# MoE blocks of 32 slots on four column tiles instead of 64 slots on two, and adaLN products on four column tiles

## What is computed

```python
mod = jax.nn.silu(cond) @ P['ada_w'][l] + P['ada_b'][l]
...
_, eidx = lax.top_k(jnp.where(emask, sel, -jnp.inf), TOP_K)
...
hg = jnp.einsum('td,edf->tef', t, w_gate)
hu = jnp.einsum('td,edf->tef', t, w_up)
act = jax.nn.silu(hg) * hu * comb[:, :, None].astype(t.dtype)
return jnp.einsum('tef,efd->td', act, w_down).reshape(B, L, D)
```

## Time and profile before

| what | value |
|---|---|
| median of the runs | 1459.06 us |
| the profiled execution: its own time, its span | 1461.17 us, 1459.5 us |
| TensorE busy | 1210.3 us, 83% of the span |
| ScalarE, VectorE busy | 341.3 us, 362.6 us |
| MoE of layer 0, first to last matmul of the loop | 385.4 to 695.1 us |
| MoE of layer 1, first to last matmul of the loop | 1080.4 to 1418.9 us |
| DRAM traffic | 352.57 MB, mean 242 GB/s |

### The profile page before, as it was taken

How to read it: one execution, slowest core, us unless ns; L and a number is a source line. 1 busy time by engine, 2 the same in 40 slices (tenths; PEclk the granted TensorE clock), 3 DMA queues, 4 the chain that set the end, 5 groups by cost and what they waited for, 6 DMA issues and landing times.

```text
span 1459.5 us, 16823 instructions
## 1 busy us (share of the span) xinstructions
PE 1210.3 (83%) x6290; PEld 645.8 (44%) x6291; DVE 362.6 (25%) x844; ACT 341.3 (23%) x577; POOL 117.2 (8%) x183
## 2 busy tenths in 40 slices
PE   1999997896499877989799999988829999897770
PEld 0444455545255444545245553443615555453330
DVE  0310138644011000111353234444301111110006
ACT  0401013303033222333221111100303333232221
POOL 1100000002100000000120000000110000000002
PEclk9999999997699998999999997999769999999985
DMA  9984333408598999987993322223173867999963
GB/s 328 363 275 173 122 123 131 159 0 348 198 380 345 391 395 393 353 330 264 379 335 115 115 71 74 100 74 115 46 286 115 316 216 288 397 381 397 388 255 129
DMA packets 93036, 352.57 MB, mean 242 GB/s; under 512 B 7270, under 2 KB 7817, under 8 KB 84812
## 3 DMA queue, kind: packets, MB, share of 16 engines
q1 hardware_dynamic: 69396, 289.16, 52.2%
q0 software_dynamic: 14736, 48.82, 10.1%
q10 hardware_dynamic: 8872, 14.16, 2.8%
HBM read 323.24 MB, written 28.87 MB: 241 GB/s over the span
## 4 chain that ended last, share of the span: by engine, by line
PE 64%; DMA 21%; DVE 8%; issue 3%; ACT 2%; SPq 1%; POOL 1%; POOLq 0%; ACTq 0%; DVEq 0%
PE bank L728 19%; DMA ring<-in_moe_w_up_dram 14%; PE bank L560 10%; PE bank L800 9%; PE bank L742 7%; PE bank L684 6%; PE bank L514 3%; DMA ring<-in_ada_w_dram 3%; DMA slot_rows<-arena,idx 2%; PE bank L722 2%; PE bank L736 1%; DMA arena<-slot_rows 1%; PE bank L873 1%; SPq L1152 1%; PE bank L896 1%
## 5 line engine op out<-in xcount | busy, mean ns | idle before, releaser
L728 PE MATMUL bank<-ring,arena 128*64 128x256 f32 x2944 | 366.4, 405 | 66.5 <-DMA ring<-in_moe_w_up_dram 54.0
L728 PEld LDWEIGHTS bank<-ring,arena 128*64 128x64 f32 x2944 | 221.2, 146 | 213.6 <-issue 128.9
L742 PE MATMUL bank<-ring,arena 128*64 128x512 f32 x736 | 175.9, 598 | 0.0
L1125 DVE TENSOR_TENSOR arena<-arena,bank 128x128 f32<-128x128 f32 x92 | 26.5, 288 | 527.2 <-ACT arena L1044 527.2
L560 PE MATMUL bank<-ring,hT 128*128 128x512 f32 x336 | 144.9, 593 | 1.0 <-ACT hT L932 1.0
L800 PE MATMUL bank<-hT,ring 128*128 128x384 f32 x384 | 124.6, 487 | 1.0 <-ACT hT L932 1.0
L514 PE MATMUL bank<-ring,small 128*64 128x512 f32 x384 | 92.0, 634 | 32.5 <-DMA ring<-in_ada_w_dram 31.7
L560 PEld LDWEIGHTS bank<-ring,hT 128*128 128x128 f32 x336 | 63.6, 190 | 80.9 <-issue 79.7
L462 POOL DMA_DIRECT2D arena<-slot_rows x96 | 50.3, 524 | 596.2 <-PE bank L722 552.3
L800 PEld LDWEIGHTS bank<-hT,ring 128*128 128x128 f32 x384 | 72.7, 190 | 52.5 <-ACT hT L932 1.2
L1042 ACT ACTIVATE arena<-bank 128x256 f32<-128x256 f32 x92 | 35.4, 385 | 223.6 <-PE bank L728 223.3
(11 more groups left out here) (275 smaller groups left out, 964.2 us busy)
## 6 DMA issues: line engine op xcount, KB each, us to landing
ring<-in_moe_w_gate_dram SPq DMA_DIRECT2D x32, 2048.0 KB, 13.7
ring<-in_moe_w_up_dram SPq DMA_DIRECT2D x32, 2048.0 KB, 20.5
ring<-in_moe_w_down_dram SPq DMA_DIRECT2D x32, 2048.0 KB, 22.6
ring<-in_ada_w_dram SPq DMA_DIRECT2D x24, 2048.0 KB, 13.8
ring<-in_ev_w_in_dram SPq DMA_DIRECT2D x7, 2048.0 KB, 13.1
arena<-slot_rows POOLq DMA_DIRECT2D x96, 128.0 KB, 6.3
ring<-in_hy_w_in_dram SPq DMA_DIRECT2D x6, 2048.0 KB, 19.7
slot_rows<-arena ACTq DMA_DIRECT2D x92, 128.0 KB, 6.2
```

Source lines behind the costliest of these rows:

```text
L728: last = pe.matmul(bank[1 + half][side * BLK:(side + 1) * BLK, 0:HALF], slot_inT[:, k % 4, k // 4, :], w[:, k, half * HALF:(half + 1) * HA ...
L742: last = pe.matmul(bank[5][half * BLK:(half + 1) * BLK, :], act_T[:, f, :], slot4(s + 2)[:, f, half * 512:half * 512 + 512], start=f == 0, ...
```

## The change

The diff, cut to its core:

```diff
-BLK = 64
+BLK = 32
...
+    for side in range(2):
+        for s in range(BLK):
+            keep[[2 * side * BLK + s, (2 * side + 1) * BLK + s], K_SIDE + side * BLK + s] = 1
...
-            for odd in range(2):
-                pool.dma_start(gates[l, n % 2, :, odd * 512:odd * 512 + 512],
-                               mod_rows[q][odd * 64:odd * 64 + 2, :]).then_inc(gate_out[n], 16)
+            for j in range(4):
+                pool.dma_start(gates[l, n % 2, :, j * HALF:j * HALF + HALF],
+                               mod_rows[q][j * 32:j * 32 + 2, :]).then_inc(gate_out[n], 16)
...
-            def row_halves(block):
-                for half in range(2):
-                    pool.dma_start(slot_in[half * BLK:(half + 1) * BLK, :],
-                                   slots[bass.ds(block * BLK, BLK), half * 512:half * 512 + 512]).then_inc(S["row_in"], 16)
+            def row_quarters(block):
+                pool.dma_start(slot_in, slots[bass.ds(block * BLK, BLK), :].rearrange("s (q c) -> q s c", q=4)).then_inc(S["row_in"], 16)
...
             for k in range(KT):
-                for odd, n in enumerate(chunks):
-                    pe.matmul(b[64 * odd:64 * odd + 64, :], condT[:, 2 * k:2 * k + 64], slot8(n)[:, k, :],
+                for j in range(4):
+                    pe.matmul(b[32 * j:32 * j + 32, 0:HALF], condT[:, 2 * k:2 * k + 32], slot8(chunks[j // 2])[:, k, j % 2 * HALF:j % 2 * HALF + HALF],
                               start=k == 0, stop=False)
...
-            def gate_and_up(s, half, k):
+            def gate_and_up(s, half, pair):
 
                 for side, w in enumerate((slot8(s), slot8(s + 1))):
-                    last = pe.matmul(bank[1 + half][side * BLK:(side + 1) * BLK, 0:HALF], slot_inT[:, k % 4, k // 4, :],
-                                     w[:, k, half * HALF:(half + 1) * HALF], start=k == 0, stop=k == KT - 1)
+                    for odd in range(2):
+                        tile = 2 * side + odd
+                        last = pe.matmul(bank[1 + half][tile * BLK:(tile + 1) * BLK, 0:HALF], slot_inT[:, odd, pair, :],
+                                         w[:, 2 * pair + odd, half * HALF:(half + 1) * HALF], start=pair == 0, stop=pair == 3)
                 return last
 
             def features(b, half):
 
                 pe.wait_ge(S["gu_out"], b * 2 + (half + 1))
-                for f in (2 * half, 2 * half + 1):
-                    last = pe.transpose(bank[3 + half][:, f % 2 * P:(f % 2 + 1) * P], gu_rows[:, f * P:(f + 1) * P], ident)
+                for f in range(2):
+                    at_f = half * HALF + f * P
+                    last = pe.matmul(bank[3 + half][:, f * 2 * BLK:(f + 1) * 2 * BLK], gu_rows[:, at_f:at_f + P], sides, start=True, stop=True)
                 last.then_inc(S["guT_mm"], 1)
 
             def down(s, f):
 
-                for half in range(2):
-                    last = pe.matmul(bank[5][half * BLK:(half + 1) * BLK, :], act_T[:, f, :],
-                                     slot4(s + 2)[:, f, half * 512:half * 512 + 512], start=f == 0, stop=f == FT - 1)
+                for q in range(4):
+                    last = pe.matmul(bank[5][q * BLK:(q + 1) * BLK, 0:HALF], act_T[:, f, :],
+                                     slot4(s + 2)[:, f, q * HALF:(q + 1) * HALF], start=f == 0, stop=f == FT - 1)
                 return last
```

More of the change, by code:

```diff
@@ L210, in trunk_program @@
         router_b = tiny(NE)
[L211 removed]
+        condT = tiny(KT * 2 + 32)
         modT = tiny(48, 2)
@@ L228, in trunk_program @@
         ffn_cols = tiny(3, rows=FH)
-        mod_rows = [ring[:, STAGING, q * 512:(q + 1) * 512] for q in range(6)]
+        mod_rows = [ring[:, STAGING, q * HALF:(q + 1) * HALF] for q in range(6)]
         cond_rows = at(18432, P, rows=16)
@@ L470, in pool_moe @@
                 pool.wait_ge(S["rowT_mm"], b)
-                row_halves(b)
-            pool.wait_ge(S["row_in"], blocks * 32 + 32)
-            pool.wait_ge(S["slot_stored"], blocks * 32 + 32)
+                row_quarters(b)
+            pool.wait_ge(S["row_in"], blocks * 16 + 16)
+            pool.wait_ge(S["slot_stored"], blocks * 16 + 16)
             pool.wait_ge(S["rowT"], blocks + 1)
@@ L512, in pe_ada @@
             for k in range(KT):
-                for odd, n in enumerate(chunks):
-                    pe.matmul(b[64 * odd:64 * odd + 64, :], condT[:, 2 * k:2 * k + 64], slot8(n)[:, k, :],
+                for j in range(4):
+                    pe.matmul(b[32 * j:32 * j + 32, 0:HALF], condT[:, 2 * k:2 * k + 32], slot8(chunks[j // 2])[:, k, j % 2 * HALF:j % 2 * HALF + HALF],
                               start=k == 0, stop=False)
-            for odd in range(2):
-                i = 12 * l + 2 * q + odd
-                last = pe.matmul(b[64 * odd:64 * odd + 64, :], ident[:, i:i + 1].to_broadcast([P, 64]), ada_bias[:, :], start=False, stop=True)
+            for j in range(4):
+                i = 12 * l + 2 * q + j // 2
+                last = pe.matmul(b[32 * j:32 * j + 32, 0:HALF], ident[:, i:i + 1].to_broadcast([P, 32]),
+                                 ada_bias[:, j % 2 * HALF:j % 2 * HALF + HALF], start=False, stop=True)
             last.then_inc(ada_mm, 1)
@@ L523, in pe_ada_columns @@
             pe.wait_ge(mod_row, ADA_ORDER.index((l, q)) + 1)
-            for j in range(4):
+            for j in range(2):
                 last = pe.transpose(b[:, j * P:(j + 1) * P], mod_rows[q][:, j * P:(j + 1) * P], ident)
@@ L748, in block_of_expert @@
                 pe.wait_ge(S["rowT"], b + 1)
-                for k in range(KT):
-                    last = gate_and_up(s, 0, k)
+                for pair in range(4):
+                    last = gate_and_up(s, 0, pair)
                 last.then_inc(S["gu_mm"], 1)
-                for k in range(4):
-                    gate_and_up(s, 1, k)
+                gate_and_up(s, 1, 0)
+                gate_and_up(s, 1, 1)
+                features(b, 0)
+                gate_and_up(s, 1, 2)
+                gate_and_up(s, 1, 3).then_inc(S["gu_mm"], 1)
                 rows_to_channels()
-                features(b, 0)
-                for k in range(4, KT):
-                    last = gate_and_up(s, 1, k)
-                last.then_inc(S["gu_mm"], 1)
+                features(b, 1)
                 pe.wait_ge(S["act"], b * 2 + 1)
@@ L762, in block_of_expert @@
                 down(s, 0)
-                features(b, 1)
                 down(s, 1)
@@ L1040, in act_moe @@
                 for half in range(2):
[L1041 to L1042 removed]
                     act.wait_ge(S["guT_mm"], b * 2 + (half + 1))
                     act.activation(silu_g[:, 2 * half:2 * half + 2, :],
[L1045 removed]
+                                   bank[3 + half][:, 0:4 * BLK].rearrange("p (f s) -> p f s", f=2)[:, :, 0:BLK],
                                    ACT.Silu).then_inc(S["silu"], 1)
[L1047 to L1049 removed]
                 act.wait_ge(S["slot_evac"], b + 2)
[L1051 to L1053 removed]
+                act.dma_start(slots[bass.ds(b * BLK, BLK), :].rearrange("s (q c) -> q s c", q=4), slot_out).then_inc(S["slot_stored"], 16)
             act.wait_ge(S["down_mm"], blocks)
@@ L1167, in load_moe @@
                             sp.wait_ge(modT_mm, 4 * (layer + 1))
-                            sp.wait_ge(gate_out[2 * layer], 32)
-                            sp.wait_ge(gate_out[2 * layer + 1], 32)
+                            sp.wait_ge(gate_out[2 * layer], 64)
+                            sp.wait_ge(gate_out[2 * layer + 1], 64)
                         else:
```

68 lines of the change are left out of this document (33 added, 35 removed).

## The result

The changed kernel took 1570.57 us in the median of 4 runs (1567.58 to 1573.15), the kernel before 1459.92 (1458.87 to 1461.1): a ratio of 1.0757, 95% interval 1.0732 to 1.0782. It is slower, as forecast, but by 111 us and not by 11, and outside the range of 1440 to 1514. The profiled execution has a span of 1565.8 us, 106.3 more than before.

A forecast was written before the change was run, and what follows sets the result against it. TensorE and DMA were taken to limit the MoE stages in turn. MoE terms of +25 us and -14 outside gave +11 on the profiled 1461.17, so 1472.4, and 2.1 lower for the median: 1470 us, range 1440 to 1514.

The forecast's parts named there:

- the price of the two row DMAs: MoE blocks: row load lands in 7.2 us beside full weight queues; store of the block before just lands at 6 to 7.
- Rival 2: MoE stages: every paced block waits for its rows at 8.5 us, +40, so 1510 us; chance 0.09.
- Block of an expert: TensorE's new block: gate/up 3.61, down 1.88, transposes 1.40, stall 0.4, in all 7.27 us where 11.83 stood.
- rivals 3 and 4: Round of four costs more than a pair: 1529 us, chance 0.07; four tiles do no more than two: 1670 us, 0.10.
- Weight loads: TensorE's gate/up and down rounds: loads overlap matmuls despite the skill's rule, so a round of four takes 0.216 us.
- Stalls where weights load: MoE: late rows make a block last 8.5 us, 1.25 more, for some 12 of 44 blocks: +15.
- Experts paced by weights: MoE experts paced by loads, 7 and 6 of them: 16.7 us for 17.4, at 392 GB/s: -9.
- Outside the MoE: adaLN pairs, column transposes, ways into and out of each MoE, routing and clock at the router: together -14 us.
- The pair (0,3): adaLN pair between TensorE's own work: takes 4.1 us where a pair took 7.95, gain -3.8.
- Edges of pairs: Where TensorE's sequencer reads the table between expert pairs: 0.8 us more shows, at some six edges: +5.
- Clock: Outside the MoE: idle TensorE may enter the first router at the lower clock: +1.5 us.
- Blocks of 32 against 64: Paced MoE blocks: 25 become 44, paying only if a block falls below 6.7 us; at 7.27 it costs +24.

The follow-up runs named there:

- both DMAs put right: Changed kernel with the row store as four DMAs and the row load as one DMA with outermost dimension 128; 1460.55 us, ratio 0.9999.
- adaLN alone: Kernel before with only the change's adaLN pairs in four column tiles, with their rows, columns and gates; experts as before; 1444.41 us, ratio 0.9881.
- DVE's order put right: Changed kernel with both DMA edits, and in DVE's queue the second gate/up half's copy moved ahead of the first half's product; 1445.04 us, ratio 0.9879.

## Why the prediction was wrong, and where it was right

**The step that failed** is the price of the two row DMAs. The prediction said of the load, "One DMA instead of two but as many packets per engine, so I take 7.2", and of the store, "the copy that stands last waits for a store of the block before, which at 6 to 7 us just lands". The load's time came from row DMAs with an outermost dimension of 64, and the store's from no row at all; the page of the kernel before has 6.2 for stores on sixteen engines. In both changed ones the outermost dimension is 4. The store runs on four engines by its packet count, with 32 pieces to an engine, and lands after 13 to 18 us beside the weights; the load takes 10.4 in the median there and 6.4 with its outermost dimension put right. The circle copy, store, copy then gives blocks of mostly 12 to 16 us, the longest 21.6, where 8.5 was the highest price in the sum. With both DMAs put right the time is 1460.55, inside the range: of the 121 us lost in the MoE stages 104 come back and 17 stay.

The Trainium skill states the rule: "DMA: Bandwidth & Descriptors", the section on why a DMA increments its semaphore by 16 and not by 1. A DMA is split over the largest number of engines up to 16 that divides the slowest dimension, of those larger than 1, on both sides. The completion packets of the stores agree, 16, 4 and 2 for outermost dimensions of 64 (or 32), 4 and 2; for the load no packet count shows it. Had I read the new DMA line for its outermost dimension and not for its bytes, a store of up to four times as long would have been a rival. Measured it was two to three times the 6.2 us of before.

Rival 2, rows as the pace, named one of the two DMAs, but at 8.5 us a block. No rival had the store, which costs more.

Term by term:

- **Block of an expert: right in sum, two terms off.** Predicted 7.27, measured 7.25. Gate/up 2.59 + 1.04 = 3.63 (3.61 predicted), down 1.86 (1.88). Twelve rounds of four in 2.59 us are 0.216 a round: four column tiles cost no more than two did, and rivals 3 and 4 are out. The other two terms miss in opposite ways, and that they cancel is luck. The 0.43 of DVE's copy in the chain is the copy and not an idle TensorE, which is at the row transposes for most of it. The timeline has 0.18 of idle before the second `features`, where 0.4 was predicted, and the ten transposes take 0.59 + 0.43 + 0.59 = 1.61 from start to start, where 1.40 was predicted:

```profile
657.19 0.44 PE L725 MATMUL bank<-keep,arena 128*128 128x128 f32 x2
657.80 0.66 PE L742 MATMUL bank<-keep,arena 128*128 128x64 f32 x4 [0.18 <-DVE arena L1122]
```

- **Weight loads: right.** The prediction set aside the rule of the Trainium skill ("TensorE: Matmul & The Clock Gate", Part 3, what overlaps and what doesn't) that a weight load overlaps running matmuls only if its row group differs. The trace differs from it on four column tiles too: 48 loads and 48 matmuls pass in the 2.59 us of twelve rounds.
- **Stalls where weights load: kind right, size too small even with both DMAs right.** 8.5 was predicted; in the version with both DMAs such blocks within an expert took 8.5 to 11.5, where the chain has stores of 8.4 to 10.2 us between copies. Two buffers took 10 us off the kernel's time. That part the prediction had at nothing ("just lands").
- **Experts paced by weights: gain too small.** Predicted 16.7 us for 17.4. In the changed kernel they took mostly 17.0 to 17.3, with the slow DMAs; with both right, gate/up starts at 485.51 and 501.28, 15.77 apart. With this and the stalls together the MoE came to +16.9 for a predicted +25.
- **Outside the MoE: right, in part by luck.** Predicted -14, measured -14.8. But adaLN alone gives 14.5 of this in its profile, so the routing and the ways in and out, put at 4, gave next to nothing in the changed kernel; in the version with both DMAs right the same stretches are 19.9 shorter. The pair (0,3) took 4.1 us from its first instruction at 113.38 to the end of its bias at 117.47, as predicted.
- **Edges of pairs: right.** 0.8 us more was to show than the 1.32 of the earlier trace rows; the timeline row at 454.67 above has 2.06, 0.74 more.
- **Clock: not in the sum.** Apart from 1.5 us at a router, the prediction had TensorE at the clock of the kernel before. Idle circles brought the mean granted clock of the first MoE from 0.95 to 0.84, and a down round at 595.47 cost about double. With both DMAs right it is 0.92.
- **Blocks of 32 against 64.** That the blocks of 32 pay only below 25/44 of the old block, 6.7 us, holds up: adaLN alone gives 1444.41, and the whole change with its DMAs and DVE's order put right 1445.04. At 7.25 us a block, the new blocks are worth nothing until the store has two buffers; with them they are worth 9 us. The old blocks were not run with two buffers. There the copy waited at most 2.5 us for anything but TensorE, so little can be expected of it.

## What to carry to other kernels

When a change rewrites a DMA's access pattern, read the new outermost dimension on both sides before its bytes: it can take a DMA from 16 engines to 4, and beside full queues the store's landing time went with the number of pieces in a row on one engine. For DMAs that ScalarE issued the packet count of its queue shows it, and the page gave no landing time for the stores on four or two engines. And when blocks are halved, look for every circle of copy, store and wait whose time does not halve with them: it was covered by the long block.

## What the runs showed of the hardware that was not expected

- Landing of a store beside full weight queues, by DMA engines used: 256 KB on two engines 31 us, 128 KB on four 13 to 18, 128 KB on sixteen 6.0 in the median from 500 to 690 us (kernel before), 32 KB on sixteen 5.8 from 500 to 700. In the version with both DMAs the last of a block's four stores still took 8.4 to 10.2 where the chain waits for it. With little else on the queues four engines were enough: from 1149 to 1178 us the changed kernel's blocks followed each other every 7.25 us.
- Four small DMAs cost the issuing engine 1.76 us where one costs 0.56. On ScalarE this delayed the silu and by way of DVE's queue TensorE, 0.29 us a block.
- DMA moved an expert's weights and rows, 6.55 MB, in 15.77 us, 415 GB/s, in the version with both DMAs, against 392 in the kernel before. Why is not shown: the row DMAs ran on sixteen engines in the kernel before, too.
- Taking away one of two limits of nearly the same height gave 42 or 27 us, taking away both 110.
